# One wide matmul for both activation parts of the last 256 tokens, joined by VectorE

## The reference

```
u = rms_norm(h, g_mix_pre)
q, k, v of 4 + 8 units = split(u @ w_in)            # 1024 x 4608: 36 column blocks
oa = chunk-band attention (8 heads of 64, 4 units of 2)
ob = differential attention (8 heads, two softmax maps, 8 units)
g_a, g_b = split(sigmoid(u @ w_gate))               # 16 column blocks
mix = (g_a * (oa @ w_branch_a) + g_b * (ob @ w_branch_b)) @ w_out
h = h + rms_norm(mix)
h = h + rms_norm(relu(rms_norm(h) @ w_up)^2 @ w_down)        # width 4096, in 4 groups
h = h + sigmoid(h @ w_ple_gate) * rms_norm(ple @ w_ple)
```

## Time and profile before

| | |
|---|---|
| median of 3 runs | 1225.08 us (1224.91 to 1225.34) |
| profiled execution, span | 1224.5 us (no other time of it is given) |
| TensorE matmul / weight load busy | 1141.7 / 1085.9 us |
| VectorE, ScalarE, GpSimd busy | 480.1, 426.8, 503.5 us |
| low weight parts (GpSimd), idle ahead of them | 585.6 us |
| high weight parts (ScalarE), idle ahead of them | 432.4 us |

### The profile page before, as it was taken

How to read it: one execution, slowest core, us unless ns; L and a number is a source line. 1 busy time by engine, 2 the same in 40 slices (tenths; PEclk the granted TensorE clock), 3 DMA queues, 4 the chain that set the end, 5 groups by cost and what they waited for, 6 DMA issues and landing times.

```text
span 1224.5 us, 22783 instructions
## 1 busy us (share of the span) xinstructions
PE 1141.7 (93%) x8318; PEld 1085.9 (89%) x8318; DVE 480.1 (39%) x908; ACT 426.8 (35%) x905; POOL 503.5 (41%) x420
## 2 busy tenths in 40 slices
PE   6119999999999999999999989999999999999897
PEld 5118898988888888999999989999999999999897
DVE  3103333355555555211244255613421530442565
ACT  6004444444544455433223234312222221223343
POOL 3023332444344443343344654544443444444551
PEclk9659999999999999999999989999999999999999
DMA  5122312222223222223222222222222222222222
GB/s 150 42 62 91 96 60 82 80 89 77 84 81 87 78 86 76 70 84 98 81 82 85 79 60 70 85 79 86 78 86 79 83 83 80 86 77 86 60 70 78
DMA packets 165538, 98.77 MB, mean 81 GB/s; under 512 B 6330, under 2 KB 161195, under 8 KB 165483
## 3 DMA queue, kind: packets, MB, share of 16 engines
q1 hardware_dynamic: 160554, 83.61, 23.6%
q0 software_dynamic: 4928, 14.42, 3.6%
HBM read 87.00 MB, written 11.01 MB: 80 GB/s over the span
## 4 chain that ended last, share of the span: by engine, by line
PE 85%; DVE 5%; DMA 4%; SPq 2%; ACT 1%; issue 1%; POOL 0%; ACTq 0%; DVEq 0%
PE proj L1353 71%; DMA band_bias<-band_sb 4%; PE turn_out L1515 3%; PE score L1433 3%; PE turn_out L1494 2%; SPq L392 2%; PE turn_out L1510 1%; DVE wide L1219 1%; PE turn_out L1465 1%; PE score L1440 1%; DMA x_tm<-x_sample 1%; DVE hT L1248 1%; ACT prob L680 1%; DVE prob L1042 1%; PE turn_out L1527 1%
## 5 line engine op out<-in xcount | busy, mean ns | idle before, releaser
L462 POOL TENSOR_TENSOR w_lo<-w_raw,w_hi 128x512 fp32r<-128x512 f32 x292 | 393.8, 1352 | 585.6 <-ACT w_hi L628 585.3
L1353 PE MATMUL proj<-act_hi,w_hi 128*128 128x288 f32 x1600 | 362.7, 308 | 60.0 <-POOL w_lo L462 51.6
L1353 PE MATMUL proj<-act_lo,w_hi 128*128 128x288 f32 x1600 | 345.0, 297 | 0.0
L1353 PE MATMUL proj<-act_hi,w_lo 128*128 128x288 f32 x1600 | 344.2, 297 | 0.0
L628 ACT ACTIVATE w_hi<-w_raw 128x512 fp32r<-128x512 f32 x292 | 182.4, 628 | 432.4 <-PE proj L1353 382.5
L1353 PEld LDWEIGHTS proj<-act_hi,w_hi 128*128 128x128 f32 x1600 | 255.8, 191 | 80.6 <-issue 68.4
L1353 PEld LDWEIGHTS proj<-act_lo,w_hi 128*128 128x128 f32 x1600 | 259.6, 190 | 0.0
L1353 PEld LDWEIGHTS proj<-act_hi,w_lo 128*128 128x128 f32 x1600 | 259.1, 190 | 0.0
L1353 PE MATMUL proj<-mid_hi,w_hi 128*128 128x288 f32 x640 | 137.4, 295 | 0.0
L1353 PE MATMUL proj<-mid_lo,w_hi 128*128 128x288 f32 x640 | 137.3, 295 | 0.0
L1353 PE MATMUL proj<-mid_hi,w_lo 128*128 128x288 f32 x640 | 137.2, 295 | 0.0
(11 more groups left out here) (203 smaller groups left out, 1076.8 us busy)
## 6 DMA issues: line engine op xcount, KB each, us to landing
w_raw<-w_in SPq DMA_DIRECT2D x72, 256.0 KB, 2.9
w_raw<-w_up SPq DMA_DIRECT2D x64, 256.0 KB, 2.7
w_raw<-w_down SPq DMA_DIRECT2D x64, 256.0 KB, 2.8
w_raw<-w_gate SPq DMA_DIRECT2D x32, 256.0 KB, 2.6
w_raw<-w_branch_b SPq DMA_DIRECT2D x16, 256.0 KB, 2.7
w_raw<-w_out SPq DMA_DIRECT2D x16, 256.0 KB, 2.8
w_raw<-w_ple_gate SPq DMA_DIRECT2D x16, 256.0 KB, 2.8
out<-k_tm POOLq DMA_DIRECT2D x12, 256.0 KB, 3.5
```

The costliest lines, as they stand in the source:

```text
L462: pool.tensor_tensor(w_lo[:, slot], w_raw[:, slot], w_hi[:, slot].bitcast(F32), ALU.subtract).then_inc(lo_done, 1)
L1353: last = pe.matmul(out[:, h], w[:, slot, at], x[:, k, HALF * h:HALF * h + HALF], start=(k == 0 and s == 0), stop=(k == blocks - 1 and s == 2))
```

## The change

The tokens are no longer cut at 288 but at C0 = 320: 320 early and 256 late ones. A k-step of most jobs (`both`) has five matmuls: first the high weights against the late tokens' high and low parts together, 2 x 256 = 512 columns, which go to two separate sums in one bank (`acc_late` and `acc_low`); then high x high early (320), low x high late (256), low x high early (320), high x low early (320). High and low parts of an activation now lie in one tensor, so that one access pattern can read both. When the job is done, VectorE copies the sum of the low parts to SBUF and adds it to the late sum (`join`), and then takes the result out as before. The jobs that ScalarE takes out (token embedding, the first six up jobs, the last gate) keep both=False: six matmuls of 256, 256, 320, 256, 320 and 320 columns, and no join. Early and late parts are next to each other across the bank border, so the result is read as one row of 576.

```diff
+        act = sb("act", [P, 2, KB, T], F32R)
+        act_hi, act_lo = act[:, 0], act[:, 1]
+        low = sb("low", [P, T - C0])
-        acc = [p[:, :].rearrange("p (h n) -> p h n", h=2)[:, :, 0:HALF] for p in proj]
+        acc = [p[:, 512 - C0:512 + T - C0] for p in proj]
+        acc_late = [p[:, 512:512 + T - C0] for p in proj]
+        acc_low = [p[:, 512 + T - C0:1024] for p in proj]
+        acc_both = [p[:, 512:1024].rearrange("p (h n) -> p h n", h=2) for p in proj]
...
+            def join(b, n):
+
+                dve.tensor_copy(low[:, :], acc_low[b]).then_inc(low_kept, 1)
+                at_least(dve, low_kept, n + 1)
+                dve.tensor_tensor(acc_late[b], acc_late[b], low[:, :], ALU.add).then_inc(joined, 1)
+                at_least(dve, joined, n + 1)
...
                 at_least(dve, w_used, u * 6 + (pieces or 2 * n + 2))
+                join(b, u * 3 + (PJ_IN + n))
                 dst = (vT, kT, qT)[n][par][:, :]
...
+            def three_products(b, hi, lo, x, k, first, final, both):
+
+                early, late = acc[b][:, 0:C0], acc_late[b]
+                if both:
+                    pe.matmul(acc_both[b], hi, x[:, :, k, C0:T], start=first, stop=False)
+                else:
+                    pe.matmul(late, hi, x[:, 0, k, C0:T], start=first, stop=False)
+                    pe.matmul(late, hi, x[:, 1, k, C0:T], start=False, stop=False)
+                pe.matmul(early, hi, x[:, 0, k, 0:C0], start=first, stop=False)
+                pe.matmul(late, lo, x[:, 0, k, C0:T], start=False, stop=final)
+                pe.matmul(early, lo, x[:, 0, k, 0:C0], start=False, stop=False)
+                return pe.matmul(early, hi, x[:, 1, k, 0:C0], start=False, stop=final)
...
-                    for s, (w, x) in enumerate(((w_hi, hi), (w_lo, hi), (w_hi, lo))):
-                        for h in range(2):
-                            last = pe.matmul(out[:, h], w[:, slot, at], x[:, k, HALF * h:HALF * h + HALF],
-                                             start=(k == 0 and s == 0), stop=(k == blocks - 1 and s == 2))
+                    last = three_products(b, w_hi[:, slot, at], w_lo[:, slot, at], x, k, k == 0, k == blocks - 1, both)
```

More of the change, by code:

```diff
@@ L122, in encoder_layer @@
     T = SEQ + SMP
-    HALF = T // 2
+    C0 = T - 256
     QB = SEQ // P + 1
@@ L1155, in gate @@
                 b = (n + PJ_GATE).mod(2)
-                dve.tensor_tensor(halves(block_of(wide, n)), acc[b], halves(x_row[:, :]), ALU.mult
+                join(b, n + PJ_GATE)
+                dve.tensor_tensor(block_of(wide, n), acc[b], x_row[:, :], ALU.mult
                                   ).then_inc(proj_free[b], 1)
@@ L1225, in _ @@
                 dve.wait_ge(w_used, PC_OUT + 2 * m + 2)
-                dve.tensor_copy(halves(mixed[:, m]), acc[b]).then_inc(proj_free[b], 1)
+                join(b, Count(PJ_OUT + m))
+                dve.tensor_copy(mixed[:, m], acc[b]).then_inc(proj_free[b], 1)
                 if m:
@@ L1284, in up_blocks @@
                         at_least(dve, w_used, group * (4 * KB) + Count(PC_FF + 2 * (first + j) + 2, [(it, RING)]))
+                        join(b, group * (2 * KB) + Count(JOINED_FF + first + j, [(it, 2)]))
                         up(Count(first + j, [(it, 2)]), acc[b],
@@ L1309, in _ @@
                 dve.wait_ge(w_used, PC_FF + (FG - 1) * 4 * KB + 2 * KB + 2 * k + 2)
-                dve.tensor_tensor(halves(down_sum[:, k]), acc[job % 2], halves(down_sum[:, k]), ALU.add
+                join(job % 2, Count(job - PJ_FF + JOINED_FF))
+                dve.tensor_tensor(down_sum[:, k], acc[job % 2], down_sum[:, k], ALU.add
                                   ).then_inc(proj_free[job % 2], 1)
@@ L1337, in wait_projection, with k_steps @@
                 at_least(pe, proj_free[b], (n + (-b)).over(2))
-            def k_steps(n, p, hi, lo, blocks=KB, input_ready=None, apart=1):
-                out = acc[n.mod(2)]
+            def three_products(b, hi, lo, x, k, first, final, both):
[9 more added lines that the diff above has]
+                return pe.matmul(early, hi, x[:, 1, k, 0:C0], start=False, stop=final)
+            def k_steps(n, p, x, blocks=KB, input_ready=None, apart=1, both=True):
+                b = n.mod(2)
                 for k in range(blocks):
@@ L1364, in unit_steps, with two_tasks @@
                 for n in range(3):
-                    yield from k_steps(u * 3 + (PJ_IN + n), u * 6 + 2 * n, act_hi, act_lo)
-            def two_tasks(n, p, ready, before, between=None):
-                tasks = [k_steps(Count(n + j), Count(p + j), act_hi, act_lo, apart=2) for j in range(2)]
+                    yield from k_steps(u * 3 + (PJ_IN + n), u * 6 + 2 * n, act)
+            def two_tasks(n, p, ready, before, between=None, both=False):
+                tasks = [k_steps(Count(n + j), Count(p + j), act, apart=2, both=both) for j in range(2)]
                 for k in range(KB):
@@ L1583, in project_ple @@
                     at = slice(2 * P * k + P * (i % 2), 2 * P * k + P * (i % 2) + P)
-                    for s, (w, x) in enumerate(((w_hi, pT_hi), (w_lo, pT_hi), (w_hi, pT_lo))):
-                        for h in range(2):
-                            last = pe.matmul(acc[n % 2][:, h], w[:, p.mod(RING), at], x[:, k, HALF * h:HALF * h + HALF],
-                                             start=(k == 0 and s == 0), stop=(k == 1 and s == 2))
+                    last = three_products(n % 2, w_hi[:, p.mod(RING), at], w_lo[:, p.mod(RING), at], pT, k, k == 0, k == 1, False)
                 last.then_inc(w_used if i % 2 else ple_first, 1)
@@ L1629, in up_blocks @@
                         project(group * (2 * KB) + Count(PJ_FF + first + j, [(it, 2)]),
-                                group * (4 * KB) + Count(PC_FF + 2 * (first + j), [(it, RING)]), act_hi, act_lo)
+                                group * (4 * KB) + Count(PC_FF + 2 * (first + j), [(it, RING)]), act)
             def down_blocks(group):
@@ L1635, in down_blocks @@
                         project(group * (2 * KB) + Count(PJ_FF + KB + j, [(it, 2)]),
-                                group * (4 * KB) + Count(PC_FF + 2 * KB + 2 * j, [(it, RING)]), mid_hi, mid_lo,
+                                group * (4 * KB) + Count(PC_FF + 2 * KB + 2 * j, [(it, RING)]), mid,
                                 input_ready=lambda k: at_least(pe, up_split, group * KB + (k + 1)))
@@ L1640, in _ @@
             late_norm(N_FPRE, PJ_FF, PC_FF)
-            up_blocks(4, KB - 4, Count(0))
+            for j in range(4, RAW):
+                project(Count(PJ_FF + j), Count(PC_FF + 2 * j), act, both=False)
+            up_blocks(RAW, KB - RAW, Count(0))
             down_blocks(Count(0))
```

59 lines of the change are left out of this document (32 added, 27 removed).

## The result

The changed kernel takes 1246.51 us (median of four runs, 1245.62 to 1247.17) against 1224.99 for the kernel before in the same series: a ratio of 1.0169 [1.0155, 1.0183]. The profiled execution has a span of 1245.3 us, 20.8 more than before's 1224.5. Slower, as forecast, but by 21.5 us where the sum said 6.9.

A forecast was written before the change was run, and what follows sets the result against it. Outside attention, TensorE's rate of six 288-column matmuls was taken to bound the kernel. Matmuls -13.6, attention joins +16.7, norms +1.9, first feed-forward group +1.9 gave +6.9 us, so 1232 us, range 1193 to 1246.

The forecast's parts named there:

- The sign: Whole kernel: the change was forecast to make it slower, chance 0.58.
- The toll of a matmul: Every five-matmul k-step: a fixed 13.3 ns per matmul and load, one saved in each of 1024 steps, -13.6 us.
- proportional rival: All k-steps: stream runs at 0.9 of full rate, nothing won per step, all joins paid; 1245.6 us, chance 18%.
- v in the B units: Attention B units: v's join delays the normalising product and the output transposes, 0.6 us in 7 units, 4.2 us.
- q at the entry of B units: Start of each attention B unit: q's join delays the combined map, 0.8 us of stall at 8 entries, 6.4 us.
- No idle time stands in this chain: VectorE's chain from q at B unit starts: no idle except a short wait for ScalarE's squares; slack 0.13 to 0.2 us.
- k, forecast 2.7 in A and nothing in B: Attention: k's join delays the last block's bias in A units, 0.67 us x4 = 2.7; in B units nothing.
- A units, q and v: Attention A units: q delays a bias that second scores wait for, 2.2 us; v 0.3 us each, 1.2 us.
- The price of a join: VectorE in each joined job: copy and add of about 430 ns each plus two waits on itself, 0.93 us.
- Norms and first group: Two norms, 2 x 0.93 = 1.9 us, and first feed-forward group, two joins before the first down job, 1.9 us.
- stalls absorbed: Rival: toll as forecast, but attention hides two thirds of its joins; 1221 us, chance 14%.
- The first rival: Every k-step: matmul length hardly depends on width up to 320, or only stream is left; some 1187 us, chance 20%.

The follow-up runs named there:

- e5: Changed kernel plus one wait: in B units GpSimd's low part of a v weight piece waits until VectorE's normalising is done; 1235.07 us, ratio 1.0067.
- e6: Kernel before with the cut at 320, six matmuls, no join, plus an unused copy and add ahead of v in B units; 1238.63 us, ratio 1.0098.
- e9_q_joins: Changed kernel with, in attention, only the q jobs' joins (k and v lose a low part) and all joins outside; 1225.52 us, ratio 0.9994.
- e4: Changed kernel with five matmuls and join only outside attention; input jobs and first three gates have six matmuls, no join; 1227.44 us, ratio 1.0001.
- e9_k_joins: Changed kernel with, in attention, only the k jobs' joins (q and v lose a low part) and all joins outside; 1232.20 us, ratio 1.0050.
- e9_v_joins: Changed kernel with, in attention, only the v jobs' joins (k and q lose a low part) and all joins outside; 1240.14 us, ratio 1.0113.
- e7: Changed kernel without five matmuls and join in attention, the last output job, first group's seventh and eighth up jobs, and last down job; 1222.96 us, ratio 0.9968.
- e1: Changed kernel with five matmuls but no joins, leaving out the low part of the last 256 tokens; 1221.95 us, ratio 0.9968.
- e3: Changed kernel with only the new cut at 320: six matmuls everywhere, no join, nothing left out; 1224.12 us, ratio 0.9986.

## Why the prediction was wrong in its size

The sign was right; the time lies half a microsecond above the range. By span the difference is +20.8 where the sum had +6.9. Step by step:

- **The toll of a matmul, forecast -13.6 us, measured -5.0.** The step that failed is "the value that the one measured width gives per matmul". I took the 13.3 ns above 288/2.4 as fixed. The starts are 117 to 119 ns behind 256 columns, 133 behind 288, 148 behind 320: 0.4625 ns a column fits all three, and only 512 columns are cheaper (232 against 237). That is the proportional rival's rate, which I had given 18%, with 5 ns a step where it said none. The earlier trace rows held nothing that could refute that rival, and half clock spoke for it: there a column takes 0.833 ns anyway, so a limit of 0.4625 can't show, while a fixed toll of 13.3 ns would have made 253 of the 240 ns. This is 8.6 us of the miss of 13.9, the largest part.
- **v in the B units, forecast 0.6 us in 7 units (4.2).** The failed step is that the product keeps its length when it starts later. It started 0.05 to 0.08 us behind GpSimd's piece and grew from 0.82 to 1.87 or 1.89 us in the seven units. TensorE waits 13.1 us there instead of 1.1 for ScalarE at the same place, and two half-clock stretches add 3.1. e5 and e6 show the cause from both sides: remove the collision and 12.4 us are gone, bring in the delay alone and 14.4 come. Without it my reasoning nearly holds: 0.8 a unit in e5.
- **q at the entry of B units, forecast 0.8 x 8 = 6.4; measured about nothing** (e9_q_joins at 0.9994; e4 at 1.0001). The failed step is "No idle time stands in this chain": the 1275 ns of the padding copy, 64x64 elements, were mostly a wait for GpSimd's piece, which stood in the groups and was overlooked. The join runs in that time, and the copy ends as late behind the start of the chain as before (2.03 us).
- **k, forecast 2.7 in A and nothing in B.** In A the wait is there, 2.9 us in 4 units. In B three of the eight entries wait 1.4 us for the combined map, which e9_k_joins shows to be k's doing. By time k costs 6.9. By the traces of e9_k_joins and e9_q_joins 4.8 of it lie in attention; the rest lies behind it, and its cause stays open.
- **A units, q and v, forecast 3.4.** A unit's period grew by 0.9 us, from 35.47 to 36.38, and k explains 0.5 of it (e9_k_joins has 35.97). v has 0.4 (35.87 in e9_v_joins); for q nothing is left. In all 3.7 us (k with them) against the 6.1 forecast.
- **The price of a join, forecast 0.93 with its waits: right.** Copy 424 and add 432 ns, 134 of each, start to start 0.45 and 0.47.
- **Norms and first group, forecast 3.8; measured 4.3.** This is the +0.6 behind attention and the 3.7 us that 752 steps gave back there. The norms paid 0.4 each and not 0.93, the first group waits 1.5 in its down job and 0.3 ahead of it. Behind the second norm the changed kernel lost 1.5 us more: it has two stretches at half clock there where before has one. e7, without the join there, is at half clock for some 10 us, and e1 and e3, without any join, for 3.4; so the join alone doesn't decide it, and what does stays open.
- **Up to the first score +0.8,** in no term of the sum: the clock rose later, with or without joins.

Attention in all: the joins cost 19.4 + 1.3 us (272 steps x 4.9 ns given back) = 20.7, not 16.7. That the two are so near is luck: v in the B units cost some 11 us more than forecast, q there 6.4 less and the A units 2.4 less, and k cost something in B units. The balance: 8.6 (rate) + 4.0 (attention) + 0.8 (start) + 0.5 (outside) = 13.9, the whole miss.

The rival "proportional rate" named 1245.6, close to the measured 1246.5. That is in part luck: its rate was nearly right, its joins were some 5 us too cheap, and its k-step 5 ns too long; the two errors cancel. The rival "stalls absorbed" is right for q alone. The first rival is refuted by the k-step.

## What to carry to other kernels

Before a matmul is merged to save weight loads, see whether the load or the stream is the longer: here a load needs 110 to 113 ns and the stream of 256 columns 118, so a load saved gave some 2 ns. When an operation on VectorE is pushed later, look at what GpSimd does at the new time, not only at the slack: a 0.9 us delay cost 1.9 at one place and nothing at another. A group whose mean is far above its size (1275 ns for 64x64 elements) was a collision here, to be understood before its neighbour is moved.

## What the runs showed of the hardware

- A VectorE product of 128x640 elements with both inputs in SBUF takes 0.82 us alone and 1.87 to 1.89 when a GpSimd product (1.26 us) started 0.05 to 0.08 us ahead of it. It goes the other way too. In the kernel before, where VectorE's sum of squares started first, GpSimd's piece took 1.81 us and not 1.27:
```profile
1112.37 0.75 DVE L1209 TENSOR_TENSOR sq_sum<-sq_sum,sq 128x576 f32<-128x576 f32 x1
...
1112.46 1.81 POOL L462 TENSOR_TENSOR w_lo<-w_raw,w_hi 128x512 fp32r<-128x512 f32 x1 [1.92 <-ACT w_hi L628]
```
  Each seems to hold the way to SBUF for its whole length. The Trainium skill (SBUF — State Buffer, "SBUF: two separate sides") says so: VectorE with two SBUF inputs and a GpSimd instruction that reads SBUF share a port pair as an exclusive lock, held by whoever starts first for the whole instruction. The trace agrees nearly: 356.17 + 1.26 is 357.43, and the blocked product ends 0.68 us after that, against 0.82 alone; the blocked piece ends 1.15 us behind the end of the sum (1113.12), against 1.27.
- A copy from SBUF to SBUF, 64x64 with one input, is hit as well: started 0.09 us into GpSimd's piece it took 1.23 us, started 1.01 us into it 0.30, and both times it ended 0.05 us behind the piece. An operation with one input in PSUM and one in SBUF is not: the taking-over of q (0.76 us) is as long beside a GpSimd piece all the way (changed kernel, 343.76) as with 0.05 us of overlap (before, 335.14).
- The start-to-start time in this data type, each matmul with its own load of 128 columns: 118 ns at 256 columns, 133 at 288, 148 at 320, 232 at 512. At 192 each narrow matmul makes some 110 ns of the k-step.
- A wait of 1.9 us in a busy stretch was followed by some 3.4 us at 1.2 GHz in two units of seven (0.57 granted over 4 us), and cost 1.55 us more each time. The trace of e6 has two such stretches too, that of e5, where the wait is 0.8, has none.
